# A two-layer encoder on one core: x loaded before the first weight tiles, squares added on VectorE, two row-product tiles moved behind the first convolution units, output in parts of 5, 5, 4 and 2 blocks

## What is computed

```python
cond = jax.nn.silu(c)
def modulation(i, s):
    mod = cond @ ada_w[i, s] + ada_b[i, s]
    shift, scale, gate = jnp.split(mod, 3, axis=-1)
h = rms_norm(x, norm_g[i, 0]) * (1.0 + scale) + shift
# layer 0, first mixer
b_gate, c_gate, v = jnp.split(h @ w_in, 3, axis=-1)
u = dwconv_centred(c_gate * v, w_conv)      # width 3
out = (b_gate * u) @ w_out
x = x + gate * out
```

## Time and profile before

| | |
|---|---|
| median of 3 runs | 2590.18 us (2588.74 to 2591.04) |
| the profiled execution | 2589.2 us, of which the span of the profile 2587.4 us |
| TensorE busy | 2535.4 us, 98% of the span |
| VectorE busy | 2091.4 us, 81% |
| ScalarE, GpSimd busy | 1376.6 us (53%), 624.5 us (24%) |
| mean granted TensorE clock | 0.994 |
| DMA over the span | 262 GB/s |

### The profile page before, as it was taken

How to read it: one execution, slowest core, us unless ns; L and a number is a source line. 1 busy time by engine, 2 the same in 40 slices (tenths; PEclk the granted TensorE clock), 3 DMA queues, 4 the chain that set the end, 5 groups by cost and what they waited for, 6 DMA issues and landing times.

```text
span 2587.4 us, 45176 instructions
## 1 busy us (share of the span) xinstructions
PE 2535.4 (98%) x15490; PEld 2245.1 (87%) x15490; DVE 2091.4 (81%) x2637; ACT 1376.6 (53%) x2152; POOL 624.5 (24%) x576
## 2 busy tenths in 40 slices
PE   7899999999999999999999999999999999999998
PEld 6799999888888888888888888888888888888887
DVE  7988898998989989758999899998799655555554
ACT  4544444544444444556777746776654444444454
POOL 0011132333343343320011142113333111121123
PEclk9999999999999999999999999999999999999999
DMA  9989997798988888746666697664588655556554
GB/s 376 416 305 375 359 372 294 275 359 313 332 331 326 331 327 327 272 154 205 213 199 200 196 370 275 202 200 153 176 288 318 200 187 187 190 184 193 187 186 140
DMA packets 163775, 678.67 MB, mean 262 GB/s; under 512 B 18705, under 2 KB 18961, under 8 KB 139057
## 3 DMA queue, kind: packets, MB, share of 16 engines
q1 hardware_dynamic: 163586, 676.71, 73.2%
q0 software_dynamic: 48, 0.13, 0.0%
HBM read 674.54 MB, written 2.23 MB: 262 GB/s over the span
## 4 chain that ended last, share of the span: by engine, by line
PE 89%; DVE 7%; DMA 2%; ACT 1%; issue 1%; POOL 0%; DVEq 0%; SPq 0%; ACTq 0%; POOLq 0%
PE psm L1197 48%; PE psm L1200 24%; PE psm L1263 3%; PE psm L1264 3%; PE psm L1265 3%; DVE wl L1522 2%; DVE adat L1535 1%; DMA xs<-in_ada 1%; PE psm L1487 1%; PE psr L1237 1%; PE psr L1403 1%; DVE xs L1535 1%; DMA raw<-in_w 1%; ACT wh L747 1%; DVE zs L1535 1%
## 5 line engine op out<-in xcount | busy, mean ns | idle before, releaser
L1522 DVE TENSOR_TENSOR wl<-raw,wh 128x1024 fp32r<-128x1024 f32 x854 | 1072.3, 1257 | 249.8 <-ACT wh L747 244.2
L747 ACT ACTIVATE wh<-raw 128x1024 fp32r<-128x1024 f32 x854 | 899.4, 1055 | 397.8 <-PE psm L1200 190.7
L1197 PE MATMUL psm<-hcat,wh 128*128 128x512 f32 x3120 | 986.3, 397 | 0.0
L1200 PEld LDWEIGHTS psm<-hcat,wl 128*128 128x128 f32 x3120 | 586.1, 188 | 138.5
L1197 PE MATMUL psm<-hid,wh 128*128 128x512 f32 x2240 | 703.6, 395 | 0.2 <-DVE wl L1522 0.2
L1200 PE MATMUL psm<-hcat,wl 128*128 128x256 f32 x3120 | 613.2, 278 | 0.0
L1200 PEld LDWEIGHTS psm<-hid,wl 128*128 128x128 f32 x2240 | 420.8, 188 | 99.5
L1197 PEld LDWEIGHTS psm<-hcat,wh 128*128 128x128 f32 x3120 | 476.1, 189 | 6.5 <-issue 5.9
L1535 DVE CUSTOM_DVE_ANT_0 adat<-adat,cond 128x2048 f32<-128x2048 f32 x176 | 463.6, 2634 | 15.6 <-ACT cond L826 9.0
L1200 PE MATMUL psm<-hid,wl 128*128 128x256 f32 x2240 | 440.1, 278 | 0.0
L1197 PEld LDWEIGHTS psm<-hid,wh 128*128 128x128 f32 x2240 | 341.0, 189 | 0.4 <-DVE wl L1522 0.4
(11 more groups left out here) (259 smaller groups left out, 2574.3 us busy)
## 6 DMA issues: line engine op xcount, KB each, us to landing
raw<-in_w SPq DMA_DIRECT2D x866, 512.0 KB, 4.5
adat<-in_ada SPq DMA_DIRECT2D x176, 1024.0 KB, 6.5
dec<-running_sums SPq DMA_DIRECT2D x48, 256.0 KB, 6.1
xs<-in_ada SPq DMA_DIRECT2D x8, 1024.0 KB, 10.6
zs<-in_ada SPq DMA_DIRECT2D x8, 1024.0 KB, 10.7
normt<-running_sums SPq DMA_DIRECT2D x16, 256.0 KB, 4.8
x<-in_xT SPq DMA_DIRECT2D x4, 512.0 KB, 7.6
out<-x SPq DMA_DIRECT2D x4, 512.0 KB, 3.5
```

The costliest lines, as they stand in the source:

```text
L747: act.activation(wh[:, h % 4, :], raw[:, h % 4, :], ACT.Copy).then_inc(hi_done, 1)
L1197: pe.matmul(both, wh[:, h % 4, (k + i) * P:(k + i + 1) * P], src[:, kb + i, :, :], start=(kb + i == 0), stop=(kb + i == KB - 1), skip_grou ...
L1200: mm = pe.matmul(bank[:, T:2 * T], wl[:, h % 4, (k + i) * P:(k + i + 1) * P], src[:, kb + i, 0, :], start=False, stop=(kb + i == KB - 1), ...
L1522: dve.tensor_tensor(wl[:, h % 4, :], raw[:, h % 4, :], wh[:, h % 4, :].bitcast(F32), ALU.subtract).then_inc(lo_done, 1)
```

## The change

On SP, the four loads of x go ahead of tile 0. On ACT, the squares of x and the Silus alternate, a square first. DVE adds the four parts of squares in three additions, so that PE sums with 4 matmuls, not 16. On DVE the reciprocal is placed between tiles 0 and 1. In the peeled step, `head_gated(4)` goes ahead of tile 33, and tile 34 goes behind `lo` of slab 39. POOL's first `keep` goes behind the second `lower`. The output is multiplied and written in parts of 5, 5, 4 and 2 blocks.

```diff
+OUT_PARTS = ((0, 5), (5, 10), (10, 14), (14, KB))
...
             def head():
                 sp.dma_start(c_row, c).then_inc(c_in, 16)
-                load_first(At(0))
                 for k in range(0, KB, 4):
                     sp.dma_start(x[:, k:k + 4, :], xT[:, k:k + 4, :]).then_inc(x_in[k // 4], 16)
+                load_first(At(0))
                 load_first(At(1))
...
                 for j in range(HEAD):
                     lower(At(j))
-                keep(At(ADA_FIRST))
+                    if j == 1:
+                        keep(At(ADA_FIRST))
...
                 for j in range(4):
+                    act.wait_ge(x_in[j], 16)
+                    act.activation(squares[j], x[:, 4 * j:4 * j + 4, :], ACT.Square).then_inc(sq_done, 4)
                     act.wait_ge(c_spread, j + 1)
                     act.activation(cond[:, j * 2 * T:(j + 1) * 2 * T], spread_bank[j][:, :], ACT.Silu).then_inc(silu_c, 1)
-                for j in range(4):
-                    act.wait_ge(x_in[j], 16)
-                    act.activation(squares[j], x[:, 4 * j:4 * j + 4, :], ACT.Square).then_inc(sq_done, 4)
...
-                for k in range(KB):
-                    at_least(pe, sq_done, 4 * (k // 4) + 4)
-                    mm = pe.matmul(psr[2][:, 0:T], ones[:, :], squares[k // 4][:, k % 4, :], start=(k == 0),
-                                   stop=(k == KB - 1), skip_group_check=True)
+                pe.wait_ge(sq_added, 3)
+                pe.wait_ge(silu_c, 3)
+                for k in range(4):
+                    mm = pe.matmul(psr[2][:, 0:T], ones[:, :], squares[0][:, k, :], start=(k == 0), stop=(k == 3),
+                                   skip_group_check=True)
...
+                for j in range(1, 4):
+                    dve.wait_ge(sq_done, 4 * j + 4)
+                    at_least(dve, sq_added, j - 1)
+                    dve.tensor_tensor(squares[0], squares[0], squares[j], ALU.add).then_inc(sq_added, 1)
                 dve.wait_ge(silu_c, 4)
-                for a in range(ADA_FIRST):
+                tile(At(0), True)
+                dve.wait_ge(rms_done, 1)
+                dve.reciprocal(rbc[:, :], rbc[:, :]).then_inc(rinv, 1)
+                tile(At(1), True)
...
                     lo(v * 2 + 7)
                     if peeled:
+                        head_gated(HEAD - 1)
                         tile(own[0])
-                        head_gated(HEAD - 1)
-                    tile(own[1])
+                    else:
+                        tile(own[1])
...
                     lo(v * 2 + 9)
+                    if peeled:
+                        tile(own[1])
                     tile(own[2])
...
-                    for k in range(0, KB, 4):
-                        at_least(dve, x_gain, k + 4)
-                        dve.tensor_tensor(x[:, k:k + 4, :], x[:, k:k + 4, :],
-                                          rbc[:, :].unsqueeze(1).to_broadcast([P, 4, T]), ALU.mult).then_inc(fin, 4)
+                    for first, after in OUT_PARTS:
+                        at_least(dve, x_gain, after)
+                        dve.tensor_tensor(x[:, first:after, :], x[:, first:after, :],
+                                          rbc[:, :].unsqueeze(1).to_broadcast([P, after - first, T]),
+                                          ALU.mult).then_inc(fin, after - first)
```

More of the change, by code:

```diff
@@ L337, in build @@
         rinv, glog, low_done, sel_done = (sem(n) for n in ("rinv", "glog", "low_done", "sel_done"))
+        sq_added = sem("sq_added")
         block = ctx.enter_context(nc.Block())
@@ L549, in norm @@
                     return
-                for k in range(4):
-                    at_least(sp, fin, 4 * (k + 1))
-                    sp.dma_start(out[:, 4 * k:4 * k + 4, :], x[:, 4 * k:4 * k + 4, :]).then_inc(out_done, 16)
+                for lo, hi in OUT_PARTS:
+                    at_least(sp, fin, hi)
+                    sp.dma_start(out[:, lo:hi, :], x[:, lo:hi, :]).then_inc(out_done, 16)
                 sp.wait_ge(out_done, 64)
@@ L1614, in scaled @@
                                       rbc[:, :].unsqueeze(1).to_broadcast([P, 4, T]), ALU.mult).then_inc(hv_done, 4)
+                for j in range(1, 4):
+                    dve.wait_ge(sq_done, 4 * j + 4)
+                    at_least(dve, sq_added, j - 1)
+                    dve.tensor_tensor(squares[0], squares[0], squares[j], ALU.add).then_inc(sq_added, 1)
                 dve.wait_ge(silu_c, 4)
-                for a in range(ADA_FIRST):
-                    tile(At(a), True)
[L1619 to L1624, removed]
-                        dve.wait_ge(rinv, 1)
-                        for k in range(4):
-                            scaled(k)
-                    if a >= 2 and a % 2 == 0:
+                tile(At(0), True)
+                dve.wait_ge(rms_done, 1)
+                dve.reciprocal(rbc[:, :], rbc[:, :]).then_inc(rinv, 1)
+                tile(At(1), True)
+                dve.wait_ge(small_in, 96)
+                dve.scalar_tensor_tensor(out=gain0[:, :], in0=modb[:, KB:2 * KB], scalar=1.0,
+                                         in1=ng_c[:, 0, :], op0=ALU.add, op1=ALU.mult).then_inc(gain0_in, 1)
+                dve.wait_ge(rinv, 1)
+                for k in range(4):
+                    scaled(k)
+                lo(At(0))
+                for a in range(2, ADA_FIRST):
+                    tile(At(a), True)
+                    if a % 2 == 0:
                         lo_part(a // 2 - 1)
-                    if a >= 1:
-                        lo(At(a - 1))
+                    lo(At(a - 1))
                 lo_part(KB - 1)
```

## The result

The changed kernel takes **2593.92 us** (median of 16 runs, 2590.36 to 2596.29) against 2588.72 us (16 runs, 2586.42 to 2591.71) for the kernel before on the same chip. The ratio is 1.0019, 95% interval 1.0011 to 1.0026: **5.2 us slower**, where 2.7 faster was forecast. The profiled execution of the changed kernel took 2590.36 us, 3.6 under its median and the lowest of the 16, so its trace shows less of the loss than the median does.

The account below looks back on a forecast made before the run. The prediction took the head's feeders (DVE, then DMA), the wait for line 1685 and the output to be what bounds PE's end; -2.0 - 1.0 + 0.3 = -2.7 us from 2590.18 gave 2587.5, range 2584.3 to 2590.9.

Parts of the forecast that it names:

- the first part: Reading of what bounds the kernel from PE's waits: almost none from 180 us on, so only three places can earn.
- three places: The head up to 142 us, PE's 3.7 us wait for line 1685, and the last microseconds behind PE.
- sign of being wrong: Listed: first square later than 7 us, gap behind a table load, DVE waiting for POOL, head ending at old time.
- The opening: Start of the kernel up to `lo` of slab 0: starts at 25.5 us instead of 27.66, 2.1 us gained.
- The sum: PE's sum of squares in the opening: 4 matmuls take 2.0 us, where 16 took 7.94.
- The rival of the late quarter of x: In the opening, x's first quarter lands at 8.8 us: +1.2 us in all, 2591.4; chance 0.05.
- the drain: Rival: two table loads on the opening's path each cost 1.38 us more: no change, 2590.2; chance 0.05.
- The head: PE's stretch up to 142 us: 2.0 us gained as the DMA queue's hole closes, bounds 0 and 2.4.
- The hole of 0.85 MB: DMA queue at 30 to 36 us, 278 GB/s against 419 later: closing it is worth 2.0 us.
- The handover: Peeled step: wait for line 1685 falls to 0.3 us, new 2.8 us wait before unit 20; 1.0 us gained (0.5 to 3.2).
- The end: Output behind PE: a first part of 5 blocks issues 0.3 us later, costing +0.3 us.
- The three terms: Head -2.0, handover -1.0 and end +0.3, together -2.7 us.

Follow-up runs that it names:

- position 0: Changed kernel plus 48 semaphore increments on PE in the head, restoring PE's code to its old place: 2587.37 us, ratio 0.9992 to the kernel before.
- +208: Kernel before plus 208 semaphore increments on PE, 13 ahead of each of the head's 16 waits: 2595.01 us, ratio 1.0018.
- +48: Kernel before plus 12 matmuls of two columns on PE behind the sum of squares: 2589.20 us, ratio 0.9996.
- +128: Kernel before plus 128 semaphore increments on PE, 8 ahead of each of the head's 16 waits: 2588.69 us, ratio 1.0001.
- +256: Kernel before plus 256 semaphore increments on PE, 16 ahead of each of the head's waits: 2590.19 us, ratio 1.0002.
- -16: Changed kernel plus 32 semaphore increments on PE, its code 16 instructions ahead of its old place: 2599.36 us, ratio 1.0040 to the kernel before.
- -32: Changed kernel plus 16 semaphore increments on PE, its code 32 instructions ahead of its old place: 2597.70 us, ratio 1.0039 to the kernel before.
- -48: Changed kernel as written, 2593.92 us, ratio 1.0019; also the kernel before with only DVE's additions and 4 sum matmuls, 2596.01 us, ratio 1.0021.

## Why the prediction was wrong

- **The step that failed** is in the first part: that behind 180 us nothing is touched, so that "the change can earn in three places only". It can earn there, but lose anywhere behind. "PE's sum is 16 matmuls in 7.94 us, so 4 take 2.0" was priced as time alone; the 48 instructions that went are also a shift of all PE's code behind them. A term is missing from the sum, 5.7 us in the profiled execution, and no rival had it. The range of 2584.3 to 2590.9 holds the changed kernel at position 0 (2587.37) and not as it was written (2593.92). No sign of being wrong that the prediction lists points at it either.
- **The opening**: `lo` of slab 0 at 25.5 was forecast and came at 25.9, in this execution. The sum, put at 2.0, took 1.99 here but 3.44 to 3.78 in four of seven traces, and then nearly all of the opening's gain is gone. The forecast takes the mean of 16 matmuls, of which before only the first few passes are 0.43 us apart; with 4 matmuls all of them can be. That term was right by luck of the execution. The first square ended 0.9 later than with a landing at 4.8, and all of the chain moved with it (reciprocal 17.46 for 16.6). The rival of the late quarter of x, which decides from 7.6 on, is out at 5.5; so is the drain. The Trainium skill (ScalarE: Activation LUTs, What ACT_TABLE_LOAD costs) has 2.66 us for a switch with its drain; here the square ends at 7.90, the load starts at 7.91 and takes 1.28, and 0.02 us behind it the Silu starts at 9.21: the drain isn't seen, and the measurement decides.
- **The head**: right in kind, 1.4 us for 2.0. The hole of 0.85 MB did close, but 30 to 36 us now moves 386 GB/s, not 419, and the opening itself won less. The hole gave back less than the 1.7 us by which the opening had moved.
- **The handover**: line 1685 was put at 165.35 in the times of before; with the head's 1.4 that is 163.95, and 163.89 came. The wait left is 0.2 (0.3), the new one 2.3 (2.8), with 3.4 us of half clock behind it, 1.7 lost (2.2). At the `lo` of slab 40 the handover is worth 2.6 - 1.4 = 1.2, where 0.7 was forecast. At unit 21, where 1.0 was forecast, PE is 3.4 us ahead, 2.0 of it by the handover, but from 250 us on it is 2.5 to 2.6, so 1.2 again; what takes the 0.9 between was not looked into.
- **The end**: the first output issue is at 2581.12, 3.37 behind the reciprocal, for 3.10 before: +0.3, as forecast.

The three terms as measured make -1.4 - 1.2 + 0.3 = -2.3; the kernel at position 0 is 2.4 faster in the medians. That they agree proves little: the terms are those of one execution with the short sum, and the trace at position 0 has the long one. The order of the waits in the three places was read rightly. What was not looked at is the rest of the program, for what hangs on the place of its code and not on its work.

**Left open**: single executions of one kernel differ by 3 to 6 us, partly by half clock stretches that come in one and not in another (24.9, 117.1, 168.3 and 1782.8 us before; 19.8, 115.4, 173.4 and 794.6 after), and what decides that was not tried. So shares under 1 us are read from traces alone, and the opening's own one isn't in any median. That the second pause differs at one position (0.65 and 2.03, and none at +208) isn't explained either.

## What to carry to other kernels

An edit that adds or removes instructions on an engine moves all its code behind; where a loop's body is nearly as long as what the engine holds, that decides whether the jump back is free or costs time, here 5 to 11 us in the medians. Count the packets of the instruction queue before and after each edit: if they differ by more than the edit's own share, look for a pause at a jump back, and price the edit again with a filling that nobody waits for. And before a difference between two traces is put down to an edit, look for it in the traces of other kernels with the same part: the 1.74 us of the late root looked like a price of the filling, and came without it too.

## What the runs showed of the hardware

- **Code position.** The body of a loop of some 1,630 instructions on PE ran its second pass without one fetch at positions 0, +48, +128 and +256, and with 9 fetches of 16 KB at -16, -32, -48 and +208. The first pause was 3.25 to 4.04 us and ended 2.96 to 3.04 us behind the start of a fetch, the second was up to 4.31, and the half clock that came with them lasted 3.4 to 10.2 us in all. The Trainium skill (Runtime: NRT & Kernel Launch, Instruction fetch mechanics) gives PE 128 KiB or 2,048 instructions, filled in order in blocks of 256, and has a taken branch stall when its target isn't in "the current 2-page window". The runs agree with the block of 256 (208 is like -48) and with the stall. They differ on the window: on PE a jump back over 7 blocks found its target held, and the measurement decides. An estimate from that page: 2,048 instructions are 8 blocks, and 8 blocks of body with the one fetched ahead behind the loop's end are 9, one too many. How many blocks are held was measured only as 7 of body yes, 8 no.
- **Names in the profile.** The pause is put down to a finished `lo` in PE's row, and to issue in that of its weight loads. In the kernel 32 short, both say issue.
- **One sum, two durations.** Behind a pause of 2.2 us or 2.3 the same 4 matmuls took 1.99 us in some executions and 3.44 to 3.78 in others, from the same start (14.9 us).
- **Instructions that cost nothing to be seen.** 256 semaphore increments on PE, ahead of waits: ratio 1.0002 (0.9992 to 1.0012). Twelve matmuls of two columns behind the sum: 0.9996 (0.9987 to 1.0005).
